# Sorting 64 experts by token count on the chip, with 96-slot experts paired to 32-slot ones, in a one-core diffusion step

## The chip, the cores and the metric

The kernel runs on one core of a Trainium2 chip. The metric is the time of one execution in microseconds (us), measured on the device. A shorter time is better.

## What is computed

One trunk layer of a diffusion backbone on 384 tokens (128 of context, 256 latent) of width 1024: a token mixer, then a mixture of experts, then a final norm. The change touches the mixture of experts alone. Everything is float32.

```python
scores = sigmoid(t @ w_router)                      # 384 x 64
idx = top 8 of (scores + bias), from the best 4 of 8 expert groups
w = scores[idx] / sum(scores[idx]) * 2.5
hid = silu(t @ we_g[e]) * (t @ we_u[e])             # 64 experts, hidden width 256
routed = sum over the 8 chosen e of  w[e] * (hid[e] @ we_d[e])
out = routed + shared expert (the same form, every token)
```

Each expert's weights are three matrices of 1 MB. The router gives 384 x 8 = 3072 token-expert pairs, 48 for each expert on average. For the inputs that the reference draws, the five fullest experts have 73, 70, 70, 66 and 65 tokens, the sixth has 63, and the five emptiest have 27 to 30. These counts follow from the reference and its inputs alone.

## The kernel before

**Mixer.** The first 360 us compute the mixer. SyncE (SP) loads 2 MB pieces of weights into a ring in SBUF, and TensorE works through them. A list of PSUM tiles (`psum_tiles`) fixes TensorE's order and which engine empties each tile; `bank(name)` asserts that order and waits for the tile that held the bank before.

**From the router to the first expert.** TensorE computes the logits, `choose` on VectorE selects eight experts for each token (`sel_ready`), and then come these steps: "rank" (a token's place among those of its expert, by matmuls with a triangular matrix) and "count" (tokens of each expert), `rankT` (ranks turned round, experts on partitions), and `slots_ring(0)` and `slots_ring(1)`, where `spread_rows` spreads the ranks of two experts over two halves of 64 partitions. `picks` on VectorE compares them with the slot number (`slotT`, a one-hot matrix of 128 slots by 384 tokens), gets each slot's token number (`idx`), and GpSimd gathers these rows of `h2_rows` by an indirect DMA (`gather`, L520, 1088 floats for a token: 1024 of the hidden state and its 64 weights). The shared expert (L895, L909, L902) is cut into pieces that fill TensorE between these steps.

**An expert pair (stage p, PAIRS = 32 of them).** Experts 2p and 2p+1 take 64 slots each. TensorE does `gate_up` (L1038, 32 matmul records), the transposes of the next pair's tokens (`tokens_of`, L985 and L988), the ranks of the pair after that (`slots_of`, L940), the transposes of the hidden values (`hidden_T`, L1050, reading every second column of `hid`), the `scatter` of the previous pair (L1072, three bf16 parts of the output times `slotT`), and `down` (L1065). VectorE computes `hid` (L1920), does `picks` for pair p+2, adds six scattered tiles to the sum in SBUF (`sums`, L1929) and splits the output in bf16 parts (`rest`, L1938, L1944), with ScalarE (L1408, L1411).

**The weight ring.** Four slots of one expert each, two pairs. SP loads the first four experts while the mixer and the router still run (`first_expert`), since experts 0 to 3 come first whatever the router says. After that it waits for `gate_up_done` of pair p-2 and issues gate and up of pair p, then for `down_done` of pair p-2 and issues down (L411, L412, L418).

**Overflow.** Experts with more than 64 tokens give further items of 32 slots. A table of items is built on the chip ("start", "items", "shift", `mine`, `ahead`). Two items make a stage of their own: TensorE splits gate from up, and the halves of down, over four groups of 32 columns (`gate_up_duo` L1102, `down_duo` L1109, `scatter_duo_tile` L1116). DUOS = 3 such stages are unrolled after the 32 pairs (LAST = 35), each with its own waits for `picks_of_duo` (L1958, L1960). More items, if any, go through a loop on all engines (`further_rounds`). An item that the table lacks loads nothing (`load_item`), but its stage is computed.

After the last `sums` VectorE adds the residual and does the final norm (L2030 to L2039).

## Time and profile before

| | us |
|---|---|
| median of 3 runs (lowest, highest) | 1014.65 (1014.25, 1015.02) |
| the profiled execution, its own time | 1012.07 |
| its span, first to last instruction | 1010.2 |
| TensorE busy | 961.8 (95%) |
| VectorE busy | 525.9 (52%) |
| ScalarE busy | 220.5 (22%) |
| mean granted TensorE clock | 0.992 |

The time of the profiled execution is its span and 1.87 us around it. "Busy" counts instructions of an engine that overlap in time once. A wait names the engine or DMA that came last. "Granted clock" is the share of 2.4 GHz at which TensorE ran.

### The profile page before, as it was taken

To read this page: it belongs to the slowest core of one execution; us is meant where nothing else is said; L and a number is where in the kernel's file an instruction comes from. 1 tells how busy PE (TensorE), PEld (TensorE's weight loads), DVE (VectorE), ACT (ScalarE), POOL (GpSimd) and SP (SyncE) were. 2 spreads that over 40 slices of the span, in tenths; PEclk is the share of its full clock that TensorE was granted. 3 is DMA by queue.
4 is the path that set the end of the run, shared out by engine and by line. 5 is a ranking of instruction groups with operands and counts; after the bars stand their busy time and mean duration, and the time that the engine had idled before them with its cause. 6 is when DMAs were issued, how large, how long until landed. Compare 5 with 4: busy or idle time off the path is not lost. (4 is left out here: it accounts for less than half of the span.)

```text
span 1010.2 us, 11595 instructions
## 1 busy us (share of the span) xinstructions
PE 961.8 (95%) x4287; PEld 450.8 (45%) x4322; DVE 525.9 (52%) x1091; ACT 220.5 (22%) x423; POOL 55.0 (5%) x71
## 2 busy tenths in 40 slices
PE   4999999999999999899999999999999999999891
PEld 2446445755655547634334343433434343343440
DVE  3203510985695944635454554545455454545666
ACT  4203002010000034212322222232222223222222
POOL 1010000100000000010000000000000000000000
PEclk9999999999999999999999999999999999999997
DMA  9992223108465369169999999999999999999931
GB/s 335 391 338 83 84 83 136 63 12 293 168 227 177 145 264 382 36 242 419 423 420 420 420 420 419 420 418 418 412 420 420 421 412 412 411 420 408 370 117 64
DMA packets 66587, 301.57 MB, mean 299 GB/s; under 512 B 6992, under 2 KB 7176, under 8 KB 39392
## 3 DMA queue, kind: packets, MB, share of 16 engines
q1 hardware_dynamic: 59376, 281.19, 69.6%
q0 software_dynamic: 7152, 19.60, 5.2%
q8 instruction: 36, 0.59, 0.2%
q14 instruction: 23, 0.19, 0.1%
HBM read 303.54 MB, written 3.80 MB: 304 GB/s over the span
## 5 line engine op out<-in xcount | busy, mean ns | idle before, releaser
L1038 PE MATMUL bank<-ring,QK 128*64 128x512 f32 x1024 | 225.2, 592 | 0.0
L1038 PEld LDWEIGHTS bank<-ring,QK 128*64 128x64 f32 x1024 | 73.5, 137 | 146.4 <-issue 146.4
L1929 DVE TENSOR_TENSOR hT<-bank,hT 128x512 f32<-128x512 f32 x210 | 129.3, 683 | 3.7 <-PE bank L1116 2.3
L1072 PE MATMUL bank<-Fm,VG 128*128 128x512 bf16 x544 | 123.2, 379 | 5.3 <-DVE S L1960 3.3
L1065 PE MATMUL bank<-ring,VG 128*64 128x512 f32 x512 | 116.9, 598 | 0.5 <-ACT VG L1401 0.5
L665 PE MATMUL bank<-ring,hT 128*128 128x512 f32 x240 | 103.8, 593 | 0.0
L1920 DVE SCALAR_TENSOR_TENSOR VG<-VG,cw,bank 128x256 f32<-128x256 f32 x32 | 15.4, 480 | 143.3 <-issue 136.9
L1938 DVE TENSOR_TENSOR Fm<-bank,Fm 128x512 f32<-128x512 f32 x64 | 44.3, 692 | 84.8 <-ACT Fm L1408 82.7
L672 PE MATMUL bank<-hT,ring 128*128 128x384 f32 x256 | 85.4, 487 | 0.0
L1072 PEld LDWEIGHTS bank<-Fm,VG 128*128 128x128 bf16 x576 | 56.3, 98 | 65.2 <-DVE S L1960 4.8
L1408 ACT CAST Fm<-bank 128x512 bf16<-128x512 f32 x64 | 37.5, 586 | 208.2 <-PE bank L1065 208.2
L665 PEld LDWEIGHTS bank<-ring,hT 128*128 128x128 f32 x240 | 45.4, 190 | 56.9 <-issue 56.3
L1065 PEld LDWEIGHTS bank<-ring,VG 128*64 128x64 f32 x512 | 33.9, 136 | 68.6 <-issue 68.0
L672 PEld LDWEIGHTS bank<-hT,ring 128*128 128x128 f32 x256 | 48.3, 190 | 34.5 <-issue 1.7
L1390 ACT ACTIVATE VG<-bank 128x256 f32<-128x256 f32 x35 | 13.4, 384 | 167.4 <-PE bank L1038 163.1
L1944 DVE TENSOR_TENSOR Fm<-Fm 128x512 bf16<-128x512 f32 x64 | 43.9, 686 | 2.8
L672 PE MATMUL bank<-Fm,ring 128*128 128x384 f32 x128 | 42.6, 486 | 0.0
L854 PE MATMUL bank<-ring,U 128*128 128x512 f32 x96 | 42.1, 594 | 0.0
L1411 ACT CAST Fm<-Fm 128x512 bf16<-128x512 f32 x64 | 39.7, 620 | 7.7 <-DVE Fm L1938 7.7
L1395 ACT COPY QK<-bank 128x512 f32<-128x512 f32 x70 | 37.6, 589 | 8.0 <-PE bank L985 8.0
L1310 ACT ACTIVATE S<-bank 128x384 f32<-128x384 f32 x16 | 7.7, 491 | 124.5 <-PE bank L672 124.5
L1472 DVE SCALAR_TENSOR_TENSOR AB<-ring,condr,AB 128x512 f32<-128x512 f32 x42 | 31.6, 752 | 1.5
(364 smaller groups left out, 892.4 us busy)
## 6 DMA issues: line engine op xcount, KB each, us to landing
ring<-in_w_exp_gate SPq DMA_DIRECT2D x69, 1024.0 KB
ring<-in_w_exp_up SPq DMA_DIRECT2D x69, 1024.0 KB
ring<-in_w_exp_down SPq DMA_DIRECT2D x69, 1024.0 KB
ring<-in_w_ada SPq DMA_DIRECT2D x12, 2048.0 KB, 10.6
ring<-in_w_in SPq DMA_DIRECT2D x10, 2048.0 KB, 16.9
ring<-in_w_four_out SPq DMA_DIRECT2D x2, 2048.0 KB, 8.1
ring<-in_w_out SPq DMA_DIRECT2D x2, 2048.0 KB, 11.3
ring<-in_w_ret_out SPq DMA_DIRECT2D x1, 2048.0 KB, 13.8
```

The source lines that it names most:

```text
L665: ins = mm(o[:, :], h[:, k, t * P:(t + 1) * P], w[:, k, :], start=(k == 0), stop=(k == KC - 1))
L672: ins = mm(o[:, 0:T], w[:, k, m * P:(m + 1) * P], rhs[:, k, :], start=(k == 0), stop=(k == kc - 1))
L854: ins = mm(o[:, :], mergedT[:, k, t * P:(t + 1) * P], w[:, k, :], start=(k == 0), stop=(k == KC - 1))
L1038: ins = mm(ps[0][n * SLOTS:(n + 1) * SLOTS, :], xT[:, k, n * SLOTS:(n + 1) * SLOTS], expert(2 * s + n)[0][:, k, :, :], start=(k == 0), sto ...
L1065: ins = mm(ps[2 + h][n * SLOTS:(n + 1) * SLOTS, :], hidT[:, j, n * SLOTS:(n + 1) * SLOTS], expert(2 * s + n)[1][:, j, h * 512:(h + 1) * 51 ...
L1072: ins = mm(ps[banks[g]][:, :], slotT[:, k, t * P:(t + 1) * P], y[:, h * 512:(h + 1) * 512], start=(n == 0), stop=(n == 2))
L1395: nc.scalar.copy(halves[n], ps[4 + n][:, :].rearrange("p (k s) -> p k s", k=4)).then_inc(sem("xT_ready"), 1)
L1408: nc.scalar.copy(y_hi[:, h * 512:(h + 1) * 512], ps[2 + h][:, :]).then_inc(sem("hi_ready"), 1)
L1411: nc.scalar.copy(y_mid[:, h * 512:(h + 1) * 512], y_rest[:, h * 512:(h + 1) * 512]).then_inc(sem("mid_ready"), 1)
L1929: v.tensor_tensor(into, o, into, ALU.add).then_inc(sem("summed"), 1)
L1938: v.tensor_tensor(y_rest[:, cut], ps[2 + h][:, :], y_hi[:, cut], ALU.subtract).then_inc(sem("rest_ready"), 1)
L1944: v.tensor_tensor(y_lo[:, cut], y_rest[:, cut], y_mid[:, cut], ALU.subtract).then_inc(sem("lo_ready"), 1)
```

## The change

Seven parts, most of them in the mixture of experts:

1. **Sort.** VectorE makes a key 64 x count - number for each expert, counts how many keys are greater (`key_rank`), and writes a permutation matrix `perm` (experts by places). The 27 pairs of the middle come first, then the five fullest, each paired with one of the five emptiest (UNEVEN = 5). A new PSUM tile "order" gives the expert of each place in one row (`tab_order`, integers for SP) and, on all partitions, the expert of each slot (`expert_at`). `spread_rows` takes `perm_bf` in place of the identity.
2. **96 and 32 slots.** Pairs 27 to 31 give three groups of 32 columns to the full expert and one to the empty one (`parts_of`). Their matmuls come as four of 32 columns instead of two of 64.
3. **No unrolled overflow stages.** LAST = 32. Items over an expert's room go through the loop of `further_rounds`, which runs only if there are any.
4. **Loads after the order is known.** `first_expert` is gone; SP waits for all mixer pieces and `order_ready`, and for every pair reads two expert numbers from `tab_order` into registers (TENSOR_LOAD) before it issues the pair's loads.
5. **Contiguous `hid`.** VectorE writes even and odd hidden columns apart (it reads `sg` and the PSUM bank in steps of two), and `hidden_T` reads contiguous blocks.
6. **Weights of a pair.** Two copies (L1950) become one operation that picks the column of `expert_at`.
7. **Order.** The shared expert's su2 matmuls (L895) and VectorE's `shared_hidden(2)` go ahead of "rank".

```diff
-DUOS = 3
-LAST = PAIRS + DUOS
+LAST = PAIRS
+UNEVEN = 5
...
-    out.extend([("rank", "V"), ("count", "V"), ("su2", "S"), ("shT0", "A"), ("rankT", "A"), ("shT1", "A"), ("shT2", "A"),
-                ("slots0", "V"), ("slots1", "V"), ("sd00", "V"),
+    out.extend([("su2", "S"), ("rank", "V"), ("count", "V"), ("shT0", "A"), ("rankT", "A"), ("shT1", "A"), ("shT2", "A"),
+                ("order", "V"), ("slots0", "V"), ("slots1", "V"), ("sd00", "V"),
...
-            first_expert(2, ("gate_up", "down"))
...
-            first_expert(3, ("gate_up", "down"))
-            first_expert(0, ("gate_up",))
-            first_expert(0, ("down",))
-            first_expert(1, ("gate_up", "down"))
...
-            for p in range(2, LAST + 1):
+            pieces_done(sp, 0, NSLOT * EXPERT)
+            sp.wait_ge(sem("order_ready"), 1)
+            for p in range(PAIRS):
                 s = p % 2
+                e = [sp.value_load(column(tab_order, 2 * p + n), min_val=0, max_val=E - 1) for n in range(2)]
+                if p >= 2:
+                    sp.wait_ge(sem("gate_up_done"), p - 1)
                 for n in range(2):
+                    load_gate_up(sp, e[n] * P, 2 * s + n, f"gate_up_slot{s}")
+                if p >= 2:
+                    sp.wait_ge(sem("down_done"), 2 * (p - 1))
                 for n in range(2):
+                    load_down(sp, e[n] * P, 2 * s + n, f"down_slot{s}")
...
+            o = bank("order")
+            pe.wait_ge(sem("perm_ready"), 1)
+            mm(o[0:1, 0:E], cols[0:E, 8:9], perm[:, :], start=True, stop=True)
+            even = PAIRS - UNEVEN
+            for q in range(4):
+                out, number = o[q * 32:(q + 1) * 32, E:E + PAIRS], cols[0:E, 8:9].broadcast_to([E, 32])
+                mm(out[:, 0:even], number, perm[:, q // 2:2 * even:2], start=True, stop=True)
+                ins = mm(out[:, even:PAIRS], number, perm[:, 2 * even + q // 3:E:2], start=True, stop=True)
...
+            def parts_of(p):
+                if p < PAIRS - UNEVEN:
+                    return [(n, slice(n * SLOTS, (n + 1) * SLOTS)) for n in range(2)]
+                return [(q // 3, slice(q * FSLOTS, (q + 1) * FSLOTS)) for q in range(4)]
...
-                    for n in range(2):
-                        ins = mm(ps[0][n * SLOTS:(n + 1) * SLOTS, :], xT[:, k, n * SLOTS:(n + 1) * SLOTS], expert(2 * s + n)[0][:, k, :, :],
+                    for n, rows in parts_of(p):
+                        ins = mm(ps[0][rows, :], xT[:, k, rows], expert(2 * s + n)[0][:, k, :, :], start=(k == 0), stop=(k == KC - 1))
...
-                    ins = nc.tensor.transpose(ps[1][:, j * P:(j + 1) * P], hid[:, j:ED:2], ident)
+                    ins = nc.tensor.transpose(ps[1][:, j * P:(j + 1) * P], hid[:, j * P:(j + 1) * P], ident)
...
+            link(v.scalar_tensor_tensor(key_ahead, key_row, 1.0, ident[0:E, 0:E], ALU.mult, ALU.mult))
+            link(v.tensor_reduce(key_col, key_ahead, AX.X, ALU.add))
+            link(v.tensor_scalar(key_ahead, key_row, key_col, None, ALU.is_gt))
+            link(v.tensor_reduce(key_rank, key_ahead, AX.X, ALU.add))
+            v.tensor_scalar(perm[:, :], const("order", E), key_rank, None, ALU.is_equal).then_inc(sem("perm_ready"), 1)
...
+            o = tile("order")
+            v.tensor_copy(tab_order[:, :], o[0:1, 0:E]).then_inc(sem("order_ready"), 1)
...
-                v.scalar_tensor_tensor(hid, sg, cw[:, k:k + 1], ps[0][:, ED:2 * ED], ALU.mult, ALU.mult).then_inc(sem("hid_ready"), 1)
+                v.scalar_tensor_tensor(turned_order(hid), by_parity(sg), cw[:, k:k + 1], by_parity(ps[0][:, ED:2 * ED]), ALU.mult, ALU.mult).then_inc(sem("hid_ready"), 1)
```

SP, from the last mixer loads into the first loads of pair 2. Before (tile_done is TensorE's count of mixer tiles; L411, L412 and L418 are gate, up and down of an expert):

```order
L411 DMA ring<-in_w_exp_gate 128x2048 [waits tile_done]
L412 DMA ring<-in_w_exp_up 128x2048
L418 DMA ring<-in_w_exp_down 128x2048 [waits tile_done]
L468 DMA QK<-in_w_shared_up 128x2048 [waits tile_done]
L469 DMA QK<-in_w_shared_down 128x1024
L411 DMA ring<-in_w_exp_gate 128x2048 [waits tile_done]
```

And now, where the same loads are L423, L424 and L430:

```order
L470 DMA QK<-in_w_shared_up 128x2048 [waits tile_done]
L471 DMA QK<-in_w_shared_down 128x1024
L485 TENSOR_LOAD tab_order [waits tile_done,order_ready]
L485 ISA x2
L485 TENSOR_LOAD tab_order
L485 ISA x2
L423 ISA
L423 DMA ring<-in_w_exp_gate 128x2048
L424 DMA ring<-in_w_exp_up 128x2048
```

No expert load stands ahead of the wait for `order_ready` any more, and each pair has two register loads ahead of its transfers.

TensorE, between the last shared gate matmuls and the slots. Before (L895 shared hidden, L951 rank, L955 count, L909 shared transposes, L962 rankT, L940 slots):

```order
L895 MATMUL bank<-Fm,hT 128x256 x7
L951 MATMUL bank<-sel_bf,cbf 128x64 [waits emptied_S,sel_ready,cbf_ready]
L951 MATMUL bank<-sel_bf,cbf 128x64 x5
L955 MATMUL bank<-cbf,sel_bf 64x1 [waits emptied_A]
L955 MATMUL bank<-cbf,sel_bf 64x1 x2
L895 MATMUL bank<-QK,hT 128x256 [waits emptied_G,shared_in]
L895 MATMUL bank<-QK,hT 128x256 x7
```

And now (L897 shared hidden, L954 rank, L958 and L960 count, L972 to L977 order, L942 slots):

```order
L897 MATMUL bank<-QK,hT 128x256 [waits emptied_S,shared_in]
L897 MATMUL bank<-QK,hT 128x256 x7
L954 MATMUL bank<-sel_bf,cbf 128x64 [waits emptied_A,sel_ready,cbf_ready]
...
L972 MATMUL bank<-perm,consts_sb 1x64 [waits perm_ready,emptied_G]
L976 MATMUL bank<-perm,consts_sb 32x27
L977 MATMUL bank<-perm,consts_sb 32x5
...
L942 MATMUL bank<-U,perm_bf 64x384 [waits emptied_S,rankT_ready,perm_ready]
```

The eight su2 matmuls now stand ahead of the wait for `sel_ready`, and nine small matmuls with a wait for `perm_ready` stand ahead of the slots.

VectorE, the chain from the rank tile to the integer table, now:

```order
L1863 SCALAR_TENSOR_TENSOR DT<-bank,DT 128x192 [waits tile_done]
L1868 COPY work<-bank 64x1 [waits emptied_V,tile_done]
L1869 SCALAR_TENSOR_TENSOR work<-bank,consts_sb 64x64 [waits vec_chain]
L1871 SCALAR_TENSOR_TENSOR work<-work,consts_sb 64x64 [waits emptied_V]
L1872 TENSOR_REDUCE work<-work 64x1 [waits vec_chain]
L1873 TENSOR_SCALAR work<-work 64x64 [waits vec_chain]
L1874 TENSOR_REDUCE work<-work 64x1 [waits vec_chain]
L1875 TENSOR_SCALAR perm<-consts_sb,work 64x64 [waits vec_chain]
```

Before, three small operations (L1864 to L1866) stood behind the count copy, and nothing waited for them until "start".

## Rows read from the trace of the kernel before

**Rows 1.** The page, part 2: GB/s of DMA in 40 slices of the span.

```profile
GB/s 335 391 338 83 84 83 136 63 12 293 168 227 177 145 264 382 36 242 419 423 420 420 420 420 419 420 418 418 412 420 420 421 412 412 411 420 408 370 117 64
```

**Rows 2.** Windows: stretch, its us, busy us by engine, granted clock, DMA share, GB/s.

```profile
443.00:463.00 20.00, 18.69 (x91) 7.20 (x92) 8.89 (x21) 4.73 (x9) 2.03 (x2) 1.00 1.01 422
463.73:913.79 450.06, 448.58 (x2159) 176.88 (x2185) 234.60 (x476) 115.88 (x224) 27.77 (x28) 1.00 1.01 418
922.00:925.00 3.00, 1.92 (x13) 0.93 (x10) 2.50 (x7) 0.89 (x3) 0.35 (x1) 1.00 0.87 325
950.00:960.00 10.00, 8.69 (x89) 4.52 (x80) 8.43 (x19) 2.87 (x6) 0.99 (x1) 1.00 0.99 367
```

**Rows 3.** Timeline of one pair: start us, us, engine, line, operation, count.

```profile
479.81 7.04 PE L1038 MATMUL bank<-ring,QK 128*64 128x512 f32 x32
487.36 0.48 DVE L1920 SCALAR_TENSOR_TENSOR VG<-VG,cw,bank 128x256 f32<-128x256 f32 x1 [4.42 <-issue]
488.08 0.51 PE L1050 MATMUL bank<-consts_sb,VG 128*128 128x128 f32 x2
495.88 1.46 PE L1038 MATMUL bank<-ring,QK 128*64 128x512 f32 x6
```

**Rows 4.** Timeline of the last two pairs and the overflow stages.

```profile
913.79 7.04 PE L1038 MATMUL bank<-ring,QK 128*64 128x512 f32 x32
...
931.44 7.04 PE L1038 MATMUL bank<-ring,QK 128*64 128x512 f32 x32
...
949.21 3.66 PE L1102 MATMUL bank<-ring,QK 128*32 128x256 f32 x64
...
983.88 1.92 PE L1109 MATMUL bank<-ring,VG 128*32 128x512 f32 x16
988.83 0.82 PE L1116 MATMUL bank<-Fm,VG 128*128 128x512 bf16 x3 [3.02 <-DVE Fm L1983]
...
989.69 3.93 DVE L1929 TENSOR_TENSOR hT<-bank,hT 128x512 f32<-128x512 f32 x6 [0.92 <-PE bank L1116]
```

**Rows 5.** DMA issues by line: operation, count, KB each.

```profile
ring<-in_w_exp_gate SPq DMA_DIRECT2D x69, 1024.0 KB
```

**Rows 6.** Timeline of TensorE from the router to pair 0.

```profile
405.84 3.62 PE L895 MATMUL bank<-Fm,hT 128*128 128x256 f32 x16
...
412.69 5.41 PE L895 MATMUL bank<-QK,hT 128*128 128x256 f32 x16
...
419.22 0.51 PE L940 MATMUL bank<-U,ident_bf 64*64 64x384 bf16 x4
...
427.90 0.66 PE L985 MATMUL bank<-consts_sb,VG 128*128 128x128 f32 x4
...
433.56 7.09 PE L1038 MATMUL bank<-ring,QK 128*64 128x512 f32 x32
```

**Rows 7.** Window of the router's end, columns as in rows 2.

```profile
415.00:420.00 5.00, 4.92 (x24) 3.84 (x23) 0.74 (x2) 1.63 (x5) 0.00 (x0) 0.80 0.00 0
```

**Rows 8.** Timeline of SP's queue: a fixed address, then one behind register loads.

```profile
440.69 0.33 SPq L411 DMA_DIRECT2D ring<-in_w_exp_gate  x1
...
922.57 0.37 SPq L411 DMA_DIRECT2D ring<-in_w_exp_gate  x1
```

**Rows 9.** Gathers (L520): first issue, all times to landing, the wait for one.

```profile
422.14 1.16 POOL L520 DMA_INDIRECT VG<-h_rows,idx  x1 [8.09 <-issue]
...
DMA to landing us min/median/max: 2.1/8.8/10.3
...
454.62 0.66 PE L985 MATMUL bank<-consts_sb,VG 128*128 128x128 f32 x4 [1.26 <-DMA VG<-h_rows,idx]
```

**Rows 10.** A small VectorE step; weight loads of two lines (count, ns min/median/max).

```profile
412.31 0.22 DVE L1823 TENSOR_REDUCE work<-S 128x1 f32<-128x64 f32 x1
...
L985 PEld LDWEIGHTS bank<-consts_sb,VG x72: 137/140/143, 427.9 to 965.6; 128*128 128x128 f32 x72
...
L1050 PEld LDWEIGHTS bank<-consts_sb,VG x70: 195/205/220, 441.9 to 979.7; 128*128 128x128 f32 x70
```

More of the change, by code:

```diff
@@ L83, in constants @@
             p % SLOTS + 1, p % FSLOTS + 1, p, p % 32 == 0, p % 32 == 1, 0 * p + 1,
-            *[np.where(p // FSLOTS % 2 == h, p % FSLOTS + 1, 1e6) for h in range(2)]]
+            *[np.where(p // FSLOTS % 2 == h, p % FSLOTS + 1, 1e6) for h in range(2)], p % (P - FSLOTS) + 1]
+    e = a(E)
+    parts["key"] = np.tile(-e[None], (P, 1))
+    far = a(UNEVEN)
+    order = np.concatenate([a(UNEVEN, E - UNEVEN), np.stack([far, E - 1 - far], 1).ravel()])
+    parts["order"] = np.tile(order[None], (P, 1))
+    room = np.where(e < E - 2 * UNEVEN, SLOTS, np.where(e % 2 == 0, P - FSLOTS, FSLOTS))
+    parts["room"] = np.tile(room[None], (P, 1))
     parts["cols"] = np.stack([np.asarray(c, float) for c in cols], 1)
@@ L347, in trunk_kernel @@
         round_at = rg[0:1, 800:800 + FURTHER]
+        key_row, key_ahead = rg[0:E, 864:928], rg[0:E, 928:992]
+        key_col, key_rank, cap, surplus = [rg[0:E, n:n + 1] for n in (992, 993, 994, 995)]
         tab = DTf[0:1, TT * E:TT * E + 2 * P + 1].bitcast(I32)
@@ L602, in gather_next @@
                 pool.wait_ge(sem("tokens_done"), q * 2 + 2 * LAST)
-                gather(pool, 1, KEEP, "gathered1")
+                gather(pool, NEXT, KEEP, f"gathered{NEXT}")
             further_rounds(pool, gather_next)
@@ L954, in _ @@
             for t in range(TT):
-                ins = mm(o[0:E, 0:1], sel_bf[:, t, :], cbf[:, 1, 0:1], start=(t == 0), stop=(t == TT - 1))
+                mm(o[0:E, 0:1], sel_bf[:, t, :], cbf[:, 1, 0:1], start=(t == 0), stop=(t == TT - 1))
+            for t in range(TT):
+                ins = mm(o[0:E, E:2 * E], cbf[:, 1, 0:E], sel_bf[:, t, :], start=(t == 0), stop=(t == TT - 1))
             done(ins)
-            shared_hidden("su", su_w, 2)
             shared_T(0)
@@ L1025, in slots_of @@
                     last_in(6)
-                spread_rows(ps[6], ident_bf, 2 * p, 2, rankT_bf).then_inc(sem("slots_done"), 1)
+                if p < PAIRS - UNEVEN:
+                    ins = spread_rows(ps[6], perm_bf, 2 * p, 2, rankT_bf)
+                else:
+                    for q in range(4):
+                        at = 2 * p + q // 3
+                        ins = mm(ps[6][q * 32:(q + 1) * 32, 0:T], perm_bf[:, at:at + 1].broadcast_to([E, 32]), rankT_bf, start=True, stop=True)
+                ins.then_inc(sem("slots_done"), 1)
+            def parts_of(p):
+                if p < PAIRS - UNEVEN:
+                    return [(n, slice(n * SLOTS, (n + 1) * SLOTS)) for n in range(2)]
+                return [(q // 3, slice(q * FSLOTS, (q + 1) * FSLOTS)) for q in range(4)]
             def gate_up(p):
@@ L1063, in down @@
                     for j in range(2):
-                        for n in range(2):
-                            ins = mm(ps[2 + h][n * SLOTS:(n + 1) * SLOTS, :], hidT[:, j, n * SLOTS:(n + 1) * SLOTS],
-                                     expert(2 * s + n)[1][:, j, h * 512:(h + 1) * 512], start=(j == 0), stop=(j == 1))
+                        for n, rows in parts_of(p):
+                            ins = mm(ps[2 + h][rows, :], hidT[:, j, rows], expert(2 * s + n)[1][:, j, h * 512:(h + 1) * 512],
+                                     start=(j == 0), stop=(j == 1))
                     ins.then_inc(sem("down_done"), 1)
@@ L1075, in tokens_next @@
             def tokens_next(q):
-                pe.wait_ge(sem("gathered1"), q * 16 + (gathered + 16))
+                pe.wait_ge(sem(f"gathered{NEXT}"), q * 16 + (gathered + 16))
                 pe.wait_ge(sem("summed"), q * 6 + 6 * (LAST + 1))
                 stand_alone(pe, "pe_passed")
-                for ins in tokens(1, ps[4], ps[5]):
+                for ins in tokens(NEXT, ps[4], ps[5]):
                     ins.then_inc(sem("tokens_done"), 1)
@@ L1947, in pair_weights @@
                 dve.wait_ge(sem(f"gathered{p % 2}"), 16 * (p // 2 + 1))
-                for n in range(2):
-                    half = slice(n * SLOTS, (n + 1) * SLOTS)
-                    v.tensor_copy(cw[half, 0:1], xg[p % 2][half, D + 2 * p + n:D + 2 * p + n + 1]).then_inc(sem("weights_ready"), 1)
+                v.scalar_tensor_tensor(picked[:, 0:E], const("item")[:, 0:E], expert_at[:, p:p + 1], xg[p % 2][:, D:ROW],
+                                       ALU.is_equal, ALU.mult, accum_out=cw[:, 0:1]).then_inc(sem("weights_ready"), 2)
                 dve.wait_ge(sem("weights_ready"), 2 * (p + 1))
```

160 lines of the change are left out of this document (66 added, 94 removed).

## The prediction, made before the changed kernel had run

> **What bounds the kernel now.** I read the slices first, then the timeline of one pair, then the end and the start of the expert part.
>
> In the slices [rows 1] DMA runs at about 420 GB/s from slice 19 to slice 36, the expert pairs. So the loads could be the bound. The windows [rows 2] say how near they are: over the 28 pairs from 463.73 to 913.79 us DMA moved 418 GB/s at a busy share of 1.01, and TensorE was busy for 448.58 of 450.06 us. Both look full. The timeline of a pair [rows 3] shows which sets the pace. A pair takes 495.88 - 479.81 = 16.07 us, TensorE hardly idles in it [rows 2], and the only wait of TensorE for a DMA in the whole expert part is the 1.26 us for gather 2 [rows 9], none for weights. TensorE is the bound, and the transfers follow it. A pair's bytes are 2 x 3 x 1.049 MB of weights and a gather of 96 rows of 4352 bytes (0.42 MB), 6.71 MB together. At 422 GB/s, the rate of 443 to 463 us when a backlog was certain [rows 2], that is 15.9 us. At 418 GB/s it is 16.05 us. There is only 0.0 to 0.2 us of slack a pair, which matters for everything below.
>
> The end [rows 4]: pair 31 starts at 931.44, the first overflow stage at 949.21, and the last sums end at 989.69 + 3.93 = 993.62. The rest, to 1010.2, is residual and norm. The DMA table [rows 5] has 69 gate loads, 64 experts and 5 overflow items. They are the five experts with more than 64 tokens.
>
> **The change, part by part.**
>
> *Overflow stages, removed.* The fullest experts have 65 to 73 tokens, under 96, the emptiest five 27 to 30, under 32, and the sixth has 63, under 64. So no item is left and the loop runs no round. Before, 993.62 - 931.44 = 62.2 us lie between the start of pair 31 and the last sums [rows 4]. After, pair 31 is a stage whose down ends 16.07 us after its start [rows 3], plus about 0.3 us because its scatter uses banks in plain order (a guess from the scatter of that form, which starts later in its stage). Then comes the split of the output, 988.83 - (983.88 + 1.92) = 3.0 us, and scatter and sums, 993.62 - 988.83 = 4.8 us [rows 4]. That is 24.2 us. Saved: **38.0 us**. Pair 30 keeps its 931.44 - 913.79 = 17.65 us, for the ranks of one overflow stage (the loop's) are still prepared there.
>
> *The start, loads.* TensorE's su2 matmuls move ahead of the rank. Before, they took 5.41 us [rows 6], in a stretch with a granted clock of 0.80 [rows 7]: TensorE had idled before it. Sixteen equal records took 3.62 us at full clock [rows 6]. I expect rank at 405.84 + 2 x 3.62 = 413.1 us, and about 0.4 us later VectorE begins. Nine dependent small steps of 0.22 us and some 0.03 us between them [rows 10] make 2.3 us, the nine order matmuls about 1.3 us, a copy 0.2 us: `order_ready` near 417.5. Then two register loads. Before, a pair's gate load behind register loads was issued at 922.57, where TensorE ended gate and up at 913.79 + 7.04 = 920.83 [rows 4, 8], 1.7 us, while a fixed one came at 440.69, with no such gap [rows 8]. First issue at 419.2, first bytes near 420.5. Gate and up of pair 0 (4.2 MB and a gather) land after 11 us, at 431.5. Pair 1's are there after 10.5 MB, two gathers and the 0.5 MB final gain: 11.85 MB / 0.421 = 28.1 us, at 448.6. Every later pair follows in 15.9 to 16.05 us.
>
> *The start, TensorE.* Its slots come at about 417.1, 2.1 us before the 419.22 of now [rows 6]. But gather 0 was alone on the DMA engines, and in the change it shares them with expert loads. Its issue moves from 422.14 to about 420.3 and its landing from the short end of 2.1 to 10.3 us to the median of 8.8 [rows 9]: 429 us. TensorE, which would get to these transposes at 427.90 - 2.1 = 425.8 [rows 6], waits 3 us. From them to pair 0 it is 433.56 - 427.90 = 5.66 us [rows 6]: pair 0 starts at 434.7. Gather 1 must wait for the end of sd21, just before pair 0, lands about 9.5 us later, at 444.2, and costs another 2.5 us. Pair 1 starts at about 450, after its weights (448.6). The wait of 1.26 us for gather 2 [rows 9] stays. Pair 2 starts at 467.4 instead of 463.73 us. I take **+3.7 us**; the ends are -2.1 (no gather is late) and +8 (both 10.3 us, and a lower clock behind the idle time, as in [rows 7]).
>
> *Contiguous `hid`.* A weight load of L1050 takes 205 ns, one of L985, contiguous, 140 ns [rows 10], two a pair: up to 0.13 us of 16.07. TensorE would go to 15.94 a pair, under the 16.05 of the transfers at 418 GB/s. I take **-2 us** for 30 pairs, between 0 and -4. On VectorE `hid` ends at 487.84 and the transposes start at 488.08 [rows 3], so reading in steps of two is free up to 0.24 us.
>
> *96 and 32 slots.* Four groups of 32 columns cost 3.66 us for half the columns [rows 4], against 7.04 / 2 = 3.52 for two groups of 64 [rows 3]. For 5 pairs, both products: **+0.4 us** (0 to +1.5).
>
> *At nothing.* The weight of a pair (one operation for two copies) and the register loads of later pairs. VectorE has 215 of 450 us free [rows 2], and SP waits for the next `gate_up_done` about 7 us after the last down issue. If that cover went, gate and up of a pair would be issued 1.7 us later, still 2 x 16.07 - 7.04 - 1.7 = 23 us ahead of their use, and with the queue not empty it would cost nothing.
>
> Sum: -38.0 + 3.7 - 2.0 + 0.4 = **-35.9 us**. Against the profiled execution of 1012.07 us it gives 976.2. The median of the runs is 2.58 us higher, so I forecast 1014.65 - 35.9 = **978.7 us**. A difference under 0.2% (2 us) can't be told from none.
>
> **A rule against the trace.** The windows show 418 to 422 GB/s for 470 us [rows 2]. The Trainium skill, "DMA: Bandwidth & Descriptors", section "Specifications", gives about 358 GB/s as the limit of HBM for one core. By it a pair would take 6.71 / 0.358 = 18.7 us, and the change, without its prefetch, would end some 29 x 2.7 = 78 us later, slower than before; the trace has been 17% above that limit all along, so it gets no weight beyond rival C.
>
> **Rivals.**
>
> A: *a pair gets longer.* `hid` is the one operation with a new access pattern on the path from gate and up to the transposes. If it took twice its 0.48 us [rows 3], the transposes would be 0.48 - 0.24 = 0.24 us later in each of 31 pairs, +7.5 us: 986. Or the transfers set the pace at 412 GB/s, the lowest expert slices [rows 1]: 16.3 us a pair from 448.6, pair 30 at 921, +5 us: 984. For it: no row shows a PSUM read in steps of two. Against: two elements apart is little, and the read of `sg` beside it lies in SBUF, as in L1050, whose weight load pays 65 ns for 128 columns [rows 10]; by that, 256 elements pay 0.13 us, within the 0.24. The Trainium skill, "SBUF — State Buffer", section "Door 1: The DMA port swizzle", says that PSUM is read in 8-byte lines and that a pattern which is not contiguous is much slower, for matmuls; no row here shows it for VectorE. By that page A would hold, with some 986 us.
>
> B: *the start costs nothing.* The gathers keep their short times, TensorE keeps the 2.1 us, and it gains the full 4 us on `hid`. 978.7 - 5.8 - 2 = 971.
>
> C: *slower.* The loads become the bound far below 418 GB/s. From 922 to 925 us DMA moved 325 GB/s, and from 950 to 960 us 367 [rows 2], where SP issued behind register loads [rows 8]. After the change all are issued so. For pair 30 to come 36 us late, a pair must take 16.07 + 36 / 29 = 17.3 us, a rate of 388 GB/s. At 367 GB/s it is 18.3 us a pair and 978.7 + 29 x 2.2 = 1042 us. Against: a transfer in flight doesn't know how its address came about, and with two pairs of ring the queue is never empty; in those stretches it was, by late issues.
>
> D: *items are left.* If ties in the router moved a count over its room, one round of the loop would run, in which nothing overlaps: a stage of (985.80 - 949.21) / 3 = 12.2 us and the tail of 3.0 + 4.8 [rows 4], some 20 us, 999.
>
> **How the numbers follow.** Forecast 0.66, A 0.14, B 0.12, C 0.04, D 0.03; 0.01 for no change. The range takes in the forecast's own ends (start -5.8 or +4.3, `hid` -2 or +2, groups +1.1, so 971 to 986), B, and most of A: **970 to 988**. Faster by more than 0.2%: 0.95, same 0.01, slower 0.04 (C).
>
> **What would show it.** In the new profile: 64 gate loads, not 69; no stage of the overflow's lines; DMA empty until about 420 us and full from there; pair 0 near 435 with a wait of some 3 us for gather 0, pair 1 near 450; pairs of 15.9 to 16.1 us; the last sums 24 us after the start of pair 31. I am wrong if TensorE waits for ring loads in most pairs (A or C), if `hid` takes over 0.7 us (A), or if loop rounds appear (D).

## The result, and the profile after

| | before | after |
|---|---|---|
| median of 4 runs on one chip, us (lowest, highest) | 1014.45 (1012.75, 1015.02) | 983.0 (982.16, 983.17) |
| the profiled execution | 1012.07 | 983.17 |
| its span | 1010.2 | 981.3 |
| TensorE busy | 961.8 | 933.0 |
| mean granted clock | 0.992 | 0.983 |

The ratio of the runs is 0.9692, 95% interval 0.9677 to 0.9706: 31 us faster, inside the range, 4 us over the forecast. The profiled execution of before lies at the low end of its runs, so the two profiles differ by 28.9 us. All steps below are counted in these two profiles, where the forecast was -35.9.

The slices of after, TensorE's clock and DMA (before: [rows 1]):

```profile
PEclk9999999999999999978999999999999999999997
...
GB/s 331 391 333 130 86 85 86 118 1 173 213 173 256 255 46 43 70 336 420 422 422 421 422 419 420 421 419 419 413 422 419 419 419 420 416 417 415 420 74 65
```

DMA moves little in the three slices up to 417 us (46, 43 and 70 GB/s) and is full from about 420 us, as forecast. But the clock shows a dent in slices 18 and 19 that before does not have. The DMA table has 64 gate loads where [rows 5] had 69:

```profile
ring<-in_w_exp_gate SPq DMA_DIRECT2D x64, 1024.0 KB, 13.7
```

TensorE's timeline from the router to pair 2 (before: [rows 6, 9]; L897 shared hidden, L954 rank, L972 order, L999 token transposes, L1063 gate and up, L1089 down):

```profile
407.81 3.62 PE L897 MATMUL bank<-Fm,hT 128*128 128x256 f32 x16
411.26 3.62 PE L897 MATMUL bank<-QK,hT 128*128 128x256 f32 x16
414.72 0.34 PE L954 MATMUL bank<-sel_bf,cbf 128*128 128x64 bf16 x6
417.60 0.27 PE L972 MATMUL bank<-perm,consts_sb 64*1 64x64 f32 x2 [0.89 <-DVE perm L1875]
...
430.54 1.09 PE L999 MATMUL bank<-consts_sb,VG 128*128 128x128 f32 x4 [3.82 <-DMA VG<-h_rows,idx]
440.60 7.09 PE L1063 MATMUL bank<-ring,QK 128*64 128x512 f32 x32
450.33 1.12 PE L999 MATMUL bank<-consts_sb,QK 128*128 128x128 f32 x4 [2.65 <-DMA QK<-h_rows,idx]
...
453.83 5.09 PE L1089 MATMUL bank<-ring,VG 128*64 128x512 f32 x16 [0.46 <-ACT VG L1410]
458.75 7.03 PE L1063 MATMUL bank<-ring,QK 128*64 128x512 f32 x32
...
474.76 5.75 PE L1063 MATMUL bank<-ring,QK 128*64 128x512 f32 x26
```

Both waits for a gather are there, 3.82 and 2.65 us, where 3 and 2.5 were forecast. What follows them is longer: from the transposes to pair 0 it is 10.06 us, not the 5.66 of [rows 6], and the first down takes 5.09 us, not 3.65. The wait of 1.26 us for gather 2, which the sum had kept [rows 9], is gone: from pair 1 to pair 2 it is 16.01 us. The windows say why. Stretch, us, busy us of PE, PEld, DVE, ACT, POOL, granted clock, DMA share, GB/s:

```profile
425.00:430.00 5.00, 1.71 (x10) 0.72 (x9) 2.64 (x10) 0.00 (x0) 0.00 (x0) 0.95 1.01 424
430.00:435.00 5.00, 4.46 (x13) 3.23 (x14) 0.75 (x2) 1.17 (x2) 0.00 (x0) 0.50 1.02 431
435.00:440.00 5.00, 5.00 (x7) 1.94 (x6) 0.69 (x1) 0.00 (x0) 0.00 (x0) 0.53 1.01 424
...
450.00:455.00 5.00, 4.21 (x16) 2.52 (x18) 1.33 (x4) 1.55 (x3) 0.00 (x0) 0.50 1.02 417
...
474.76:923.00 448.24, 446.77 (x2313) 174.21 (x2340) 234.41 (x476) 115.96 (x224) 27.73 (x28) 1.00 1.01 419
```

Behind each wait TensorE ran at a granted clock of 0.50, that is 1.2 of 2.4 GHz. The last row is the 28 pairs from pair 2 to pair 30, against 450.06 us in [rows 2]: still full on TensorE and on DMA.

The end, from pair 30 on (before: [rows 4]; L1096 scatter, L1952 sums):

```profile
923.00 7.05 PE L1063 MATMUL bank<-ring,QK 128*32 128x512 f32 x64
...
940.64 7.05 PE L1063 MATMUL bank<-ring,QK 128*32 128x512 f32 x64
...
960.18 3.83 PE L1096 MATMUL bank<-Fm,VG 128*128 128x512 bf16 x17 [3.03 <-DVE Fm L1967]
...
960.82 3.93 DVE L1952 TENSOR_TENSOR hT<-bank,hT 128x512 f32<-128x512 f32 x6 [0.92 <-PE bank L1096]
```

Put together, where the time went:

| stretch | before | after | change | forecast |
|---|---|---|---|---|
| to the start of pair 2 | 463.73 | 474.76 | +11.0 | +3.7 |
| pairs 2 to 29 | 450.06 | 448.24 | -1.8 | -1.6 |
| pair 30 | 17.65 | 17.64 | 0.0 | 0 |
| start of pair 31 to the last sums | 62.18 | 24.11 | -38.1 | -38.0 |
| after the last sums | 16.58 | 16.55 | 0.0 | 0 |

The one row that is off is the start, by 7.3 us. It is what the experiments are about.

### The profile page after: what moved, and what is told of

Its sections match the earlier page's. It is cut to its first block, busy times and chain, and to the rows that moved or that the text cites. A ratio compares the mean times of both kernels' runs of the same rounds, so it can differ in the third digit from the quotient of the medians.

```text
span 981.3 us, 11669 instructions
## 1 busy us (share of the span) xinstructions
PE 933.0 (95%) x4219; PEld 433.9 (44%) x4251; DVE 500.8 (51%) x1045; ACT 211.7 (22%) x405; POOL 52.0 (5%) x68
## 4 chain that ended last, share of the span: by engine, by line
PE 91%; DMA 4%; DVE 2%; ACT 1%; issue 1%; SPq 0%; DVEq 0%; POOLq 0%; ACTq 0%
PE bank L1063 22%; PE bank L674 15%; PE bank L1096 12%; PE bank L1089 12%; PE bank L667 11%; PE bank L856 4%; PE bank L999 2%; DMA ring<-in_w_in 2%; PE bank L897 2%; PE bank L690 2%; PE bank L1002 2%; PE bank L1074 1%; DMA VG<-h_rows,idx 1%; DMA QK<-h_rows,idx 1%; PE bank L942 1%; PE bank L722 1%
## 5 line engine op out<-in xcount | busy, mean ns | idle before, releaser
L1063 PE MATMUL bank<-ring,QK 128*64 128x512 f32 (+1 forms) x1184 | 225.3, 592 | 0.0
L1063 PEld LDWEIGHTS bank<-ring,QK 128*64 128x64 f32 (+1 forms) x1184 | 72.5, 130 | 147.5 <-issue 147.5
L1096 PE MATMUL bank<-Fm,VG 128*128 128x512 bf16 x544 | 122.8, 379 | 6.5 <-DVE Fm L1967 3.0
L1952 DVE TENSOR_TENSOR hT<-bank,hT 128x512 f32<-128x512 f32 x192 | 118.1, 682 | 3.7 <-PE bank L1096 2.6
L1089 PE MATMUL bank<-ring,VG 128*64 128x512 f32 (+1 forms) x592 | 118.3, 603 | 0.5 <-ACT VG L1410 0.5
L1943 DVE SCALAR_TENSOR_TENSOR VG<-VG,cw,bank 128x256 f32<-128x256 f32 x32 | 15.4, 481 | 144.5 <-issue 138.1
L1096 PEld LDWEIGHTS bank<-Fm,VG 128*128 128x128 bf16 x576 | 56.0, 98 | 66.6 <-DVE Fm L1967 3.7
L1089 PEld LDWEIGHTS bank<-ring,VG 128*64 128x64 f32 (+1 forms) x592 | 33.8, 131 | 70.2 <-issue 69.3
L1404 ACT COPY QK<-bank 128x512 f32<-128x512 f32 x64 | 34.5, 589 | 9.5 <-PE bank L999 9.2
```

The costliest lines, as they stand in the source:

```text
L1063: ins = mm(ps[0][rows, :], xT[:, k, rows], expert(2 * s + n)[0][:, k, :, :], start=(k == 0), stop=(k == KC - 1))
L1089: ins = mm(ps[2 + h][rows, :], hidT[:, j, rows], expert(2 * s + n)[1][:, j, h * 512:(h + 1) * 512], start=(j == 0), stop=(j == 1))
L1096: ins = mm(ps[banks[g]][:, :], slotT[:, k, t * P:(t + 1) * P], y[:, h * 512:(h + 1) * 512], start=(n == 0), stop=(n == 2))
L1404: nc.scalar.copy(halves[n], ps[4 + n][:, :].rearrange("p (k s) -> p k s", k=4)).then_inc(sem("xT_ready"), 1)
L1952: v.tensor_tensor(into, o, into, ALU.add).then_inc(sem("summed"), 1)
```

## The experiments

Two theories for the lost 7.3 us at the start, and a question behind them. **Theory 1**: the loads share the DMA engines with the two first gathers, TensorE waits, and its clock then falls to half; a kernel that keeps it busy, or makes the gathers early, gets the time back at the end. **Theory 2** (rival): the loads themselves are late. Without the four experts that used to be loaded under the router the ring has no lead (the time by which a pair's weights are in SBUF before TensorE wants them), and TensorE would have to wait for the loads a little later if it came earlier. The question behind: do the other terms (contiguous `hid`, slots of 96 and 32) have the size that the sum gave them?

The diffs below are against the changed kernel. "Before" of each is run on the same chip, and the ratios are to it; its medians were 1011.89 to 1013.12 us in the experiments, against 1014.45 above.

### Keep TensorE busy through the two waits

```diff
+            pe.wait_ge(sem("g2_rows_in"), 16)
+            for _ in range(4):
+                mm(lo[:, :], ident, U[:, 0:512], start=True, stop=True)
             pe.wait_ge(sem("gathered0"), 16)
...
+                if p == 1:
+                    last_in(4)
+                    for _ in range(3):
+                        mm(ps[4][:, :], ident, U[:, 0:512], start=True, stop=True)
                 pe.wait_ge(sem(f"gathered{p % 2}"), 16 * (p // 2 + 1))
```

The products of these matmuls are overwritten.

> The changed kernel, with four float32 128x512 matmuls on idle data ahead of the wait for gather 0 and three ahead of the wait for gather 1 (their results are overwritten). The waits stay as long; only the idle time goes. Theory (most of what the start cost over my sum is TensorE's half clock after the two waits, 430 to 440 us and 450 to 455 us): granted clock 1.00 in both stretches, pair 0 starts some 4 us earlier (about 436.5), pair 2 some 5.5 us earlier (about 469 instead of 474.8), time 977.5. Rival (the landing of the gathers and the DMA traffic set the start, the clock is beside the point): pair 2 stays within 1 us of 474.8 and the time within 982 to 984.

Measured: 982.58 us, ratio 0.9714 (0.9698 to 0.9730), the same as the change within what can be told. The timeline of TensorE (gate and up are L1070 here):

```profile
435.27 7.09 PE L1070 MATMUL bank<-ring,QK 128*64 128x512 f32 x32
451.52 7.09 PE L1070 MATMUL bank<-ring,QK 128*64 128x512 f32 x32 [0.75 <-DMA ring<-in_w_exp_up]
...
469.47 7.09 PE L1070 MATMUL bank<-ring,QK 128*64 128x512 f32 x32 [1.47 <-DMA ring<-in_w_exp_up]
...
616.41 7.09 PE L1070 MATMUL bank<-ring,QK 128*64 128x512 f32 x32 [1.41 <-DMA ring<-in_w_exp_up]
...
681.71 7.09 PE L1070 MATMUL bank<-ring,QK 128*64 128x512 f32 x32 [0.78 <-DMA ring<-in_w_exp_up]
...
921.92 7.05 PE L1070 MATMUL bank<-ring,QK 128*32 128x512 f32 x64
```

The clock stayed up, and pair 0 came at 435.27 (forecast: 434.7), pair 2 at 469.47, 5.3 us ahead of the change. By pair 30 only 1.1 us of that is left (921.92 against 923.00). In between stand waits that the change does not have, for the gate and up weights of the ring: 4.7 us in all. So the mechanism of theory 1 is real (pair 2 came as early as it expected), but the time is the rival's: of the 5.3 us about 1 us is left at pair 30, and 0.8 us of the 5.3 is an earlier start of this execution (its shared stage starts at 406.99 us, not 407.81). The late loads of theory 2 take the rest.

### Put sd2 ahead of the first tokens; issue gather 1 early; give gather 0 the DMA engines alone

Three more ways to take the waits for the gathers away. The first puts the shared expert's last pieces, 3.7 us of matmuls, between the issue of gather 0 and its transposes, which also frees gather 1 earlier:

```diff
+            shared_down(2, 0)
+            shared_down(2, 1)
             lo = bank("tokens0a")
             hi = bank("tokens0b")
             pe.wait_ge(sem("gathered0"), 16)
```

> The changed kernel, with the two shared down tiles sd20 and sd21 (3.6 us) ahead of the transposes that wait for gather 0, on TensorE and VectorE. Theory (the wait and the clock drop behind it are the loss): the wait of 3.8 us shrinks under 0.5 us, the clock stays 1.00, pair 0 starts near 433.5, gather 1 is issued some 10 us earlier and lands before pair 0's gate and up end, pair 1 follows near 446 or, if its weights are now late, near 449; pair 2 at 465 to 466, time about 974. Rival (ring loads are the bound at the start once the gathers are not): pair 1 waits for its weights until 449 to 451 and pair 2 starts at 467 or later, time 976 to 978.

Measured: 981.72 us, ratio 0.9700 (0.9680 to 0.9721). Both expected times (974, and 976 to 978 by the rival) are missed. Pair 0 came at 434.18, but pair 1 waited 6.05 us for its weights until 453.11. Pair 30 came at 922.16.

The second gives gather 1 a place in SBUF that is free early, so that it goes right behind gather 0 (GpSimd clears that place first):

```diff
-        xg = [VG[:, 1920:1920 + ROW], QK[:, 0:ROW]]
+        xg = [VG[:, 1920:1920 + ROW], DTf[:, 448:448 + ROW]]
...
-                if p == 1:
-                    computed(pool, "sd21")
```

> The changed kernel, with the rows of gather 1 in a buffer that is free by then (cleared by GpSimd first), so that gather 1 follows gather 0 at once and does not wait for sd21. The wait for gather 0 and the clock drop behind it stay. Theory: the wait of 2.65 us for gather 1 goes, and with it the half clock of 450 to 455 us (some 2 us): pair 2 starts 4.5 us earlier, at 470, time about 978.5. Rival (gather 1's traffic beside gather 0 delays gather 0 by as much): pair 0 starts 1 to 2 us later and the time is 980 to 983.

Measured: 984.77 us, ratio 0.9733 (0.9717 to 0.9750), above both expected times and, by its ratio, slower than the change (0.9692). The profiled execution is the fastest of the four, 983.13 us. No wait for gather 1 is left, but pair 1 still waits 1.96 us for its weights, and pairs 2, 11 and 15 wait 1.61, 1.60 and 0.85 us. Pair 30: 921.27.

The third holds back all expert loads until gather 0 has landed:

```diff
             sp.wait_ge(sem("order_ready"), 1)
+            sp.wait_ge(sem("gathered0"), 16)
```

> The changed kernel, with SyncE's first expert load held until gather 0 has landed. Theory (gather 0 is late because it shares the DMA engines with the expert loads): it lands about 4 us after its issue, near 426, TensorE waits for it not at all or under 0.5 us and keeps its clock, but the loads start 4 to 5 us later, so that pair 0 waits for its weights until about 437 and pair 1 until about 453: pair 2 near 470. Time 976 to 980. Rival (gather 0 takes 8 to 9 us whatever else runs): the wait stays near 3.8 us, all loads are 8 us later and the time rises to 988 to 991.

Measured: 986.76 us, ratio 0.9750 (0.9733 to 0.9767), where 976 to 980 or, by the rival, 988 to 991 were expected. The timeline (token transposes L1000, gate and up L1064):

```profile
424.23 0.66 PE L1000 MATMUL bank<-consts_sb,VG 128*128 128x128 f32 x4
...
439.11 9.54 PE L1064 MATMUL bank<-ring,QK 128*64 128x512 f32 x32 [9.15 <-DMA ring<-in_w_exp_up]
```

The gather did not keep TensorE waiting at all: from issue to landing it took 4.5 us, against 8.9 beside the loads in the change, which settles the sharing. But TensorE then stood 9.15 us for the first weights. SP waited 6.9 us for the gather. The first issue is at 425.19 us instead of 420.64, only 4.5 us later, because this execution's shared stage started 2.4 us earlier (405.40).

What follows from all four: the weights of a late pair, not the gathers, fix the end. Their waits end at pair 15, at 681.71, 681.8 and 681.1 us in the first three. The changed kernel, with its start some 5 us later, reaches pair 15 at 682.84 without a wait. It has fallen just behind its own loads: its last load of up for pair 1 (L424) landed 24.6 us after its issue at 427.07, 7.1 us before TensorE wanted it, and the one for pair 15 landed 22.4 us after its issue at 659.5, at 681.9, only 0.9 us before.

### Light gathers first

A pair's gather moves 4352 bytes for each of its tokens. In the sorted order that is 0.55 MB for pair 0, 0.41 MB for pair 15 and 0.27 MB for pair 26, beside 6.29 MB of weights. At 419 GB/s a pair's transfers take 16.3 us for pair 0, 16.0 for pair 15 and 15.7 for pair 26. TensorE needs 16.0. So up to about pair 15 the loads should lose ground, and from there gain. This is an estimate from bytes, and it is too small: the mean gather of pairs 2 to 15 is 0.46 MB, which gives 16.1 us a pair, while the kernel that was kept busy went from pair 2 to pair 15 in 212.24 us, 16.33 a pair. If the gathers make the waits all the same, the middle in rising order of counts moves them:

```diff
-    order = np.concatenate([a(UNEVEN, E - UNEVEN), np.stack([far, E - 1 - far], 1).ravel()])
+    order = np.concatenate([a(UNEVEN, E - UNEVEN)[::-1], np.stack([far, E - 1 - far], 1).ravel()])
```

This kernel has the edit on sd2, too.

> e2_sd2_first with the 27 middle pairs in rising instead of falling order of count, so that the first gathers move 0.27 MB instead of 0.55 MB. Theory (sorting put the heaviest gathers first, 6.84 MB or 16.25 us of transfers for a pair against TensorE's 16.0, just where the ring has no lead; so the loads, late from the start, stay the bound up to pair 15): pair 1 waits for its weights 3 us instead of 6, pairs 2 to 30 follow at 16.00 us each without a wait for the ring, pair 30 starts at 914 to 916 instead of 922.2, time 974 to 976. Rival (the waits at pairs 11 and 15 come from where those weights lie in memory or from a lower DMA rate in that stretch, not from the size of the gathers): waits of 1 to 2 us for ring loads remain, pair 30 starts at 919 to 922, time 978.5 to 982.

Measured: 982.49 us, ratio 0.9699 (0.9664 to 0.9734); the 974 to 976 us that I had expected are missed. The late waits did move:

```profile
432.01 7.09 PE L1063 MATMUL bank<-ring,QK 128*64 128x512 f32 x32 [2.10 <-DMA ring<-in_w_exp_up]
449.76 9.44 PE L1063 MATMUL bank<-ring,QK 128*64 128x512 f32 x32 [4.87 <-DMA ring<-in_w_exp_up]
...
676.26 7.04 PE L1063 MATMUL bank<-ring,QK 128*64 128x512 f32 x32
...
856.41 8.78 PE L1063 MATMUL bank<-ring,QK 128*64 128x512 f32 x32 [2.05 <-DMA ring<-in_w_exp_up]
...
922.24 7.05 PE L1063 MATMUL bank<-ring,QK 128*32 128x512 f32 x64
```

None at pairs 11 and 15, but pairs 25 and 26 wait, and pair 30 comes at the same 922. The waits that are listed are not all: TensorE went from pair 2 to pair 15 (676.26) in 16.01 us a pair, and from there to pair 26 in 180.15 us, 16.38 a pair. So TensorE is held up where the heavy gathers are, in either order, by about 4 us over the 11 or 13 pairs; why they cost more than their bytes stays open. The order of the middle decides where TensorE meets the loads, not when it is through: the bytes are the same, and they begin at the same time. That leaves the time at which the loads begin.

### Two pairs loaded early

So give the ring its lead back: the weights of experts 0 to 3 are loaded as in the kernel before, and used for pairs 0 and 1.

```diff
+            first_expert(2, ("gate_up", "down"))
             computed(sp, "ro7")
...
+            first_expert(3, ("gate_up", "down"))
+            first_expert(0, ("gate_up",))
+            first_expert(0, ("down",))
+            first_expert(1, ("gate_up", "down"))
             sp.wait_ge(sem("order_ready"), 1)
-            for p in range(PAIRS):
+            for p in range(2, PAIRS):
```

This leaves out the weights of the four experts that the sort puts in pairs 0 and 1.

> The changed kernel, with the weights of experts 0 to 3 loaded into the ring ahead of the router as in the kernel before, and used for pairs 0 and 1 whatever the order says; pairs 2 to 31 as in the changed kernel. It leaves out that pairs 0 and 1 get their own weights; gathers, slots and the amount of transfers are the same. Theory (what the start costs over the kernel before is the lost lead of the ring, by way of the gathers that now share the DMA engines and of TensorE's half clock behind their waits): no wait for gather 0, clock 1.00, pair 0 starts near 432.5, pair 2 near 463, no wait for ring loads, pair 30 near 911, time 971 to 973. Rival (sorting itself, the order tile and the longer chain, costs the start): pair 0 starts at 436 or later, time 976 or more.

Measured: 969.87 us, ratio 0.9574 (0.9539 to 0.9609), 13 us under the change. Gate and up of pairs 2 and 30:

```profile
460.85 7.04 PE L1076 MATMUL bank<-ring,QK 128*64 128x512 f32 x32
...
909.09 7.05 PE L1076 MATMUL bank<-ring,QK 128*32 128x512 f32 x64
```

No ring wait is left, gather 0 causes no wait, the pace is 16.00 to 16.01 us from pair 2 on, and pair 30 starts at 909.09. Pair 2 starts 13.9 us before that of the change and 2.9 us before that of the kernel before [rows 2], so the start of the change, with its sort and its order tile, costs nothing once the weights are there; the rival is out. Theory 2 has its price: the lost lead costs 13 us. That is the price of both of its ways together, the gathers that now share the DMA engines (with the clock behind their waits) and the weights that come late; the two overlap, and taking away the first alone gave about 1 us at pair 30. Before the change the lead was 30 us of transfers (12.6 MB), made under the end of the mixer and the router.

### The old form of hid

```diff
-                    ins = nc.tensor.transpose(ps[1][:, j * P:(j + 1) * P], hid[:, j * P:(j + 1) * P], ident)
+                    ins = nc.tensor.transpose(ps[1][:, j * P:(j + 1) * P], hid[:, j:ED:2], ident)
...
-                v.scalar_tensor_tensor(turned_order(hid), by_parity(sg), cw[:, k:k + 1], by_parity(ps[0][:, ED:2 * ED]),
+                v.scalar_tensor_tensor(hid, sg, cw[:, k:k + 1], ps[0][:, ED:2 * ED],
```

> The changed kernel with hid written and read as before, the transposes again reading every second column. Theory (TensorE's own work is the pace of a pair, 16.01 us, and the contiguous weight loads took 0.06 us from it): pairs of 16.07 us, pair 30 starts 1.8 us later after pair 2, hid takes 0.48 us as with the steps of two, time 984.5 to 985.5. Rival (the pace of 16.00 to 16.01 us is set by the loads): pairs stay at 16.01 us and the time at 983.

Measured: 985.70 us, ratio 0.9730 (0.9694 to 0.9766), 0.2 us above what the theory expected. First the windows of the 28 pairs from pair 2 on, then `hid` itself (L1943: count, ns min/median/max), both of this kernel:

```profile
474.30:924.40 450.10, 448.62 (x2312) 175.69 (x2340) 234.46 (x476) 115.89 (x224) 27.70 (x28) 1.00 1.01 419
```

```profile
L1943 DVE SCALAR_TENSOR_TENSOR VG<-VG,cw,bank x32: 479/481/482, 448.8 to 949.7; 128x256 f32<-128x256 f32 x32
```

450.10 us against 448.24 with contiguous blocks: 0.07 us a pair, so the rival (the loads set the pace) is out for this profile. The two weight loads of a pair (L1074) take 206 ns each here and 141 in the change, 0.13 us together; half of that comes through. `hid` takes 479/481/482 ns here, and the changed kernel's `hid`, which reads `sg` and PSUM in steps of two, gives the same three numbers:

```profile
L1943 DVE SCALAR_TENSOR_TENSOR VG<-VG,cw,bank x32: 479/481/482, 448.2 to 948.2; 128x256 f32<-128x256 f32 x32
```

### Three uneven pairs

With `UNEVEN = 3` the fourth and fifth fullest experts get 64 slots, and their two items go through one round of the loop.

```diff
-UNEVEN = 5
+UNEVEN = 3
```

> The changed kernel with three uneven pairs instead of five. The fourth and fifth fullest experts (66 and 65 tokens) then have 64 slots each, so two items are left and the overflow loop runs one round. Theory (my rival D: in the loop nothing overlaps, and a round costs a stage and its tail): 20 us more than the changed kernel, about 1003, with the round's loads of 6.3 MB waited for only if they take longer than the end of pair 31. Rival (the loads of a round are issued one stage ahead and only the unrolled stage's 12.2 us are paid): 995.

Measured: 1001.72 us, ratio 0.9892 (0.9856 to 0.9928), 18.7 us over the change where 20 were expected. The loop is real, does what the unrolled stages did, and runs no round in the changed kernel.

### Four experts with fixed places

The early loads need experts that are known before the router is done; the sort needs none in particular. So experts 4 to 7 get keys above all others, which puts them in places 0 to 3, and the other 60 are sorted as before. Only constants and SP's first loads change. Whatever the input, what does not fit a room goes through the loop; in this one the four have 56, 50, 33 and 48 tokens and fit 64 slots.

```diff
+FIRST = 4
...
-    parts["key"] = np.tile(-e[None], (P, 1))
+    fixed = (e >= FIRST) & (e < FIRST + NSLOT)
+    parts["key"] = np.tile(np.where(fixed, 32768 * (FIRST + NSLOT - e), -e)[None], (P, 1))
...
-    order = np.concatenate([a(UNEVEN, E - UNEVEN), np.stack([far, E - 1 - far], 1).ravel()])
+    order = np.concatenate([a(NSLOT), a(NSLOT + UNEVEN, E - UNEVEN), np.stack([NSLOT + far, E - 1 - far], 1).ravel()])
...
+                    load_gate_up(sp, (e + FIRST) * P, e, f"gate_up_slot{e // 2}")
```

> The changed kernel with experts 4 to 7 always in places 0 to 3 (by their keys; the other 60 are sorted, and the uneven pairs come from those), so their weights are loaded before the routing is known, as the four first experts of the kernel before. It computes the whole reference. Theory (the head start of the ring is what the sorted order lost, about 13 us): the pace stays 16.0 us a pair with no wait for weights, pair 0 starts at about 432, pair 31 at about 927, time 970 (968 to 973), within 1.5 us of the run that loaded experts 0 to 3 early. Rival (that run was fast because its wrong pairs happened to save gathers or waits): over 976, with waits for weights in the first pairs. Faster than both kernels in either case.

Measured: 970.33 us (969.71 to 971.39, 5 runs), ratio 0.9583 (0.9563 to 0.9603). Gate and up (L1078) of pairs 0 to 2 and of pair 30, and the windows of the 28 pairs:

```profile
429.88 7.09 PE L1078 MATMUL bank<-ring,QK 128*64 128x512 f32 x32
...
442.58 7.04 PE L1078 MATMUL bank<-ring,QK 128*64 128x512 f32 x32
...
459.61 7.04 PE L1078 MATMUL bank<-ring,QK 128*64 128x512 f32 x32
...
907.85 7.05 PE L1078 MATMUL bank<-ring,QK 128*32 128x512 f32 x64
```

```profile
459.60:907.90 448.30, 448.30 (x2344) 173.90 (x2344) 234.55 (x476) 115.90 (x224) 27.70 (x28) 1.00 1.01 419
```

TensorE is busy for every one of the 448.30 us, at a full clock. The rival (the fast run came from its wrong pairs) is out. This is 43 us under the kernel before and 13 us under the change, both run on the same chip.

### The changed kernel once more

> The changed kernel, not edited, once more. Time 982 to 984. The start of the expert part varies from run to run: if the 2 us by which the first shared stages were late in the first profile are not of the change, the first shared stage (407.8 us there) should start anywhere from 405.5 to 408 here. Pair 2 follows it at 66.5 to 67.5 us (67.0 in the first profile), since the two waits for gathers and the half clock behind them are of the kernel.

Measured: 983.61 us, ratio 0.9709 (0.9686 to 0.9733). The timeline of TensorE and one window behind the second wait:

```profile
407.31 3.62 PE L897 MATMUL bank<-Fm,hT 128*128 128x256 f32 x16
...
439.57 7.09 PE L1063 MATMUL bank<-ring,QK 128*64 128x512 f32 x32
449.16 0.66 PE L999 MATMUL bank<-consts_sb,QK 128*128 128x128 f32 x4 [2.51 <-DMA QK<-h_rows,idx]
...
471.32 7.04 PE L1063 MATMUL bank<-ring,QK 128*64 128x512 f32 x32
...
616.74 7.09 PE L1063 MATMUL bank<-ring,QK 128*64 128x512 f32 x32 [1.18 <-DMA ring<-in_w_exp_up]
...
682.00 7.09 PE L1063 MATMUL bank<-ring,QK 128*64 128x512 f32 x32 [0.77 <-DMA ring<-in_w_exp_up]
...
922.20 7.05 PE L1063 MATMUL bank<-ring,QK 128*32 128x512 f32 x64
```

```profile
450.00:455.00 5.00, 4.54 (x25) 1.68 (x25) 2.03 (x5) 1.89 (x4) 1.04 (x1) 1.00 1.00 401
```

The first half of the expectation held: the shared stage that started at 407.81 started at 407.31. It is at 405.84 in the kernel before and at 405.38 in the version with four fixed experts, whose code up to there is that of the change but for the early loads. In the profiles that load no expert early it lies between 405.40 (loads after gather 0) and 408.12 (the old form of `hid`). So the 2 us come and go between executions. The second half missed: pair 2 came 64.0 us behind that stage, not 67. The second wait was there again, 2.51 us, but this time the clock stayed at 1.00 behind it. And it made little difference: TensorE came 3.4 us earlier to pair 2, had to wait for the loads at pairs 11 and 15, and was at pair 30 0.8 us earlier. In one execution of this kernel the late start sets the end, in the other the late loads.

## Why the prediction was right, and where it was off

**Overflow stages, -38.0.** Measured -38.1. Each piece of the step is there: a last stage of the pair's length, the split of 3.03 us [rows 4 have 3.02], scatter and sums.

**Contiguous `hid`, -2, and 96 and 32 slots, +0.4.** The sum over pairs 2 to 29 came to -1.8. The run with the old `hid` gives 450.10 us for them, against 450.06 before, so the whole gain is that of `hid` and the slots of 96 and 32 cost nothing that can be seen. The -2 was a pick between 0 and -4; that it fits is partly luck. My guess of +0.4 priced 32 columns from the overflow's own form.

**The start, +3.7. This is the term that was mis-sized: +11.0.** Step by step against the forecast: the rank at 414.72 instead of 413.1 and the first load at 420.64 instead of 419.2 (the execution was already 2 us late at the shared stage, which varies by as much); the waits for the gathers 3.82 and 2.65 us instead of 3 and 2.5; but then pair 0 10.06 us behind the transposes instead of 5.66, since I copied a duration from a stretch at full clock and put it behind a wait that I had just forecast. The lower clock stood only in the end of the term's range (+8), which +11.0 passes, although [rows 7] showed a clock of 0.80 behind idle time. The half clock made the work behind the two waits 4.4 and 2.7 us longer (10.06 for 5.66, 8.42 for 5.75); the run that kept TensorE busy had pair 2 at 469.47, 5.3 us earlier, with 2.2 us of new waits for weights before it. The wait of 1.26 us for gather 2, which the forecast kept, did not occur, which hid 1.3 us of the miss.

**What the sum left out.** With the clock repaired, my chain for TensorE was right to 0.6 us (pair 0 at 435.27), and the kernel was still no faster. What failed there is the schedule of the loads. It was late from the first pairs: pair 1's weights, forecast for 448.6, landed at 451.7, 1.4 us of it from the later first issue; pair 2's, forecast for 464.6, were waited for until 468.8 and 469.5 in two runs. And "Every later pair follows in 15.9 to 16.05 us" is wrong: up to pair 15 it was 16.3 us a pair (681 to 682, where the forecast comes to 673 at most). I used a mean gather of 0.42 MB, but the sort puts the heavy pairs first; by their bytes that accounts for under 0.1 us a pair, and what makes up the rest stays open. I had written that the slack was 0.0 to 0.2 us a pair and that this matters for everything; I should have drawn from it that a lead in the ring, once lost, is not earned back. The kernel before had no wait for weights because of that lead. Losing it costs 13 us, by two kernels that bring it back (969.87 and 970.33 us). The change pays it out of the 38 us of the overflow, and the total is near the forecast because that one large term was right.

**Rivals.** A (a longer pair) did not occur by way of `hid`: it takes 481 ns, and a pair 16.00 to 16.01 us. The Trainium skill's rule in "SBUF — State Buffer", section "Door 1: The DMA port swizzle", on patterns that are not contiguous in PSUM's 8-byte lines speaks of matmuls, and does not show for this VectorE read: 481 ns in steps of two, 481 ns without. A's other way, transfers at 16.3 us a pair, 984 in all, came closer than I gave it credit for: up to pair 15 the loads came at that pace, though at 419 to 421 GB/s and not 412, and in the second profile of the same kernel TensorE waited for them. B (a start that costs nothing) is roughly what the kernel with four fixed experts reaches, 970.33 against the 971 given for it, for another reason. C (loads far below 418 GB/s) did not occur: behind register loads DMA moved 419 GB/s over the 28 pairs. The 358 GB/s for one core in the Trainium skill, "DMA: Bandwidth & Descriptors", section "Specifications", do not bind here: the windows show 419 GB/s for 448 us. D (a loop round) did not occur; one round, forced, costs 18.7 us where 20 were given.

## What to carry to other kernels

Where TensorE and the transfers are within 1 or 2% of each other, the time lost by taking away transfers that ran under the stage before (here 13 us, for 30 us of transfers) is not won back in the later pairs: ask of a change not only how long its loads take but when the first one can be issued. If data decides the order of the work, keep as many items out of the decision as the buffers hold, so that loading can begin before it is made. And never put a duration taken at full clock behind a wait of some microseconds without a second, doubled value beside it.

## What was new about the hardware

The granted clock behind a short wait is not the same in each execution, and the length of the wait alone does not tell it. After 3.82 and 3.97 us of waiting (the two profiles of the changed kernel) it fell to 0.50; after 2.65 us it fell in one, after 2.51 us it stayed at 1.00 in the other. In the profile with light gathers first it was 1.00 from 430 to 440 us, behind a wait of 2.10 us at pair 0, and 0.81 over the 8.8 us behind one of 2.05 us at pair 26. Seven filler matmuls, placed ahead of the waits, kept it at 1.00 from 425 to 460 us.

Expert loads in flight slow an indirect gather: the first one took 8.9 us from issue to landing beside the loads, 4.5 us when they were held back, and 3.7 us in the kernel before. The total did not fall: 424 and 431 GB/s in the two windows from 425 to 435 us, against 419 over the pairs behind.
